# A two-layer decoder on one core: gMLP's v first in each layer, norms by token halves, gates one branch ahead

## What is computed

```python
for l in range(DEPTH):
    h = rmsnorm(x, attn_norm_gain[l])
    q, k, v, pz, gu, gv, g = jnp.split(h @ w_in[l], SPLIT_POINTS, axis=-1)
    gates = jax.nn.sigmoid(g + b_gate[l]).reshape(B, S, N_BRANCHES, D)
    ya = sliding_window_attention(q, k, v, attn_sinks[l], rel_bias) @ w_branch_a[l]
    yb = multiscale_pool(pz, w_pool[l], pool_scale[l]) @ w_branch_b[l]
    yc = chunked_spatial_gating(gu, gv, gmlp_v_gain[l], w_spatial[l], b_spatial[l]) @ w_branch_c[l]
    x = x + (gates[:, :, 0] * ya + gates[:, :, 1] * yb + gates[:, :, 2] * yc) @ w_out[l]
    h2 = rmsnorm(x, ffn_norm_gain[l])
    x = x + peer_ffn(h2, peer_w_query[l], peer_sub_keys1[l], peer_sub_keys2[l], peer_expert_u[l], peer_expert_v[l])
return rmsnorm(x, final_gain)
```

## Time and profile before

| | us |
|---|---|
| median of 3 runs (2059.02 to 2060.73) | 2060.33 |
| the profiled execution's own time | 2059.37 |
| its span | 2057.6 |
| PE busy | 2017.3 |
| DVE busy | 1469.7 |
| ACT busy | 1057.9 |
| POOL busy | 1028.4 |

### The profile page before, as it was taken

The page is one execution under the profiler, slowest core; times in us unless marked ns, Lnnn a source line. Parts: engine busy times, 40 slices in busy tenths (PEclk is TensorE's granted clock), DMA queues, the critical chain, the costliest instruction groups (busy, mean ns, idle before and its releaser), DMA issues.

```text
span 2057.6 us, 41405 instructions
## 1 busy us (share of the span) xinstructions
PE 2017.3 (98%) x13730; PEld 1874.1 (91%) x13730; DVE 1469.7 (71%) x2984; ACT 1057.9 (51%) x1751; POOL 1028.4 (50%) x427
## 2 busy tenths in 40 slices
PE   7999999999999999999989999999999999999997
PEld 6999899999998888889889999999999988888896
DVE  3943169688887888886649341796888778888775
ACT  5644454577774333334365444546777733333343
POOL 5798679877770000004368886797777600000042
PEclk9999999999999999999999999999999999999999
DMA  7455557665667777876454554576565677787763
GB/s 260 135 185 185 173 180 228 223 199 194 196 198 227 242 240 241 242 242 218 162 186 144 187 188 169 187 229 217 195 199 195 195 238 241 241 242 240 233 215 122
DMA packets 164486, 423.36 MB, mean 206 GB/s; under 512 B 18075, under 2 KB 76620, under 8 KB 163868
## 3 DMA queue, kind: packets, MB, share of 16 engines
q1 hardware_dynamic: 163724, 418.24, 63.3%
q10 hardware_dynamic: 288, 2.10, 0.2%
q0 software_dynamic: 368, 1.57, 0.2%
HBM read 388.29 MB, written 33.55 MB: 205 GB/s over the span
## 4 chain that ended last, share of the span: by engine, by line
PE 93%; issue 2%; POOL 2%; ACT 1%; DVE 1%; DMA 0%; DVEq 0%; POOLq 0%; ACTq 0%
PE bank L1112 53%; PE bank L1313 34%; PE bank L1364 3%; POOL halves L463 2%; PE bank L1291 1%; DVE hT L792 0%; PE bank L1274 0%; PE bank L1134 0%; PE bank L1213 0%; ACT area L505 0%; DMA x<-in_x 0%; ACT halves L528 0%; DVE area L785 0%; ACT area L559 0%; PE bank L1223 0%
## 5 line engine op out<-in xcount | busy, mean ns | idle before, releaser
L463 POOL TENSOR_TENSOR halves<-ring,halves 128x1024 fp32r<-128x1024 f32 x412 | 1021.8, 2490 | 992.7 <-DVE coef L1045 617.7
L528 ACT ACTIVATE halves<-ring 128x1024 fp32r<-128x1024 f32 x668 | 705.3, 1057 | 759.5 <-PE bank L1313 408.2
L1112 PE MATMUL bank<-hT,halves 128*128 128x256 f32 x8736 | 1081.5, 283 | 10.2 <-DVE hT L792 9.3
L1112 PEld LDWEIGHTS bank<-hT,halves 128*128 128x128 f32 x8736 | 1063.8, 192 | 16.2 <-DVE hT L792 10.8
L1313 PE MATMUL bank<-halves,coef 128*128 128x512 f32 x3072 | 703.0, 389 | 0.0
L1313 PEld LDWEIGHTS bank<-halves,coef 128*128 128x128 f32 x3072 | 574.4, 188 | 118.6 <-issue 0.5
L1027 DVE TENSOR_TENSOR halves<-ring,halves 128x1024 fp32r<-128x1024 f32 x256 | 315.8, 1234 | 10.4 <-ACT halves L528 10.0
L1039 DVE TENSOR_TENSOR act<-act,area 128x256 f32<-128x256 f32 x256 | 157.5, 615 | 58.8 <-ACT act L641 55.8
L1043 DVE CAST coef<-act 128x256 fp32r<-128x256 f32 x256 | 75.4, 294 | 100.8 <-PE bank L1313 98.0
L690 ACT ACTIVATE onehot<-onehot,weight 128x128 fp32r<-128x128 f32 x256 | 89.1, 395 | 108.2 <-DVE onehot L1010 108.1
L1004 DVE TENSOR_TENSOR onehot<-bank,ids 128x512 fp32r<-128x512 f32 x128 | 88.6, 692 | 48.5 <-PE bank L1364 48.5
(11 more groups left out here) (149 smaller groups left out, 1070.6 us busy)
## 6 DMA issues: line engine op xcount, KB each, us to landing
ring<-in_stream SPq DMA_DIRECT2D x672, 512.0 KB, 3.7
held_blocks<-act SPq DMA_DIRECT2D x220, 128.0 KB, 1.8
act<-held_blocks SPq DMA_DIRECT2D x220, 128.0 KB, 2.9
area<-rel_scratch SPq DMA_DIRECT2D x2, 1024.0 KB, 6.2
x_home<-x ACTq DMA_DIRECT2D x2, 1024.0 KB, 4.2
x<-x_home SPq DMA_DIRECT2D x2, 1024.0 KB, 8.0
rel_scratch<-act POOLq DMA_DIRECT2D x1, 1532.0 KB, 14.7
area<-in_consts SPq DMA_DIRECT2D x2, 576.0 KB, 3.8
```

The lines of the kernel that those rows point to most:

```text
L463: pool.tensor_tensor(halves[:, s, 1, :], ring[:, s, :], halves[:, s, 0, :].bitcast(F32), ALU.subtract)\
L528: a.activation(halves[:, s, 0, :], ring[:, s, :], ACT.Copy).then_inc(hi_done, 1)
L1112: i = pe.matmul(o, stationary[a], moving[b], start=begin and n == 0, stop=end and n == len(TERMS) - 1)
```

## The change

- **Order of a layer.** gv comes first (tiles 2 to 5), by token halves: PE transposes half 0, starts its gv products, transposes half 1. Then k, v, q, the logits, pz, gu, and the four tiles of gate 0 where gv and gu were. After the mixers each gate runs one branch ahead (gate 1, branch 0, gate 2, branch 1, ..., gate 5, branch 4, branch 5); gate 0 has a buffer of its own.
- **Norms by halves.** DVE scales x by 1/rms and by the gain (loaded spread over all partitions, `gain_a`, `gain_f`) into `hn`; PE transposes with the identity (L1274 of the new kernel), ACT and DVE split straight from PSUM. ACT's root, DVE's scaling and PE's transposes alternate between the halves.
- **wo.** Tiles 4 to 7 run for half 0 first, then 4 to 6 for half 1, the transposes of half 0, tile 7 for half 1, five products by the identity, the transposes of half 1.
- **End of PEER.** The last two u tiles stand together, and the last three v tiles are added for half 0 first, then for half 1; the last coefficients have a buffer of their own. x is added and normed by halves here too.
- **Parameters** are no longer tiles of the stream: they are one DMA (`par`), after the bias in layer 0, before the end of the layer in layer 1. POOL makes the four masks after low half 19. The bias table is written from SP's queue, not POOL's; x arrives as two DMAs from two queues.
- **POOL waits** in layer 1 before low halves 3 and 4 until DVE has scaled half 0 and half 1.

The core of the diff:

```diff
-    [("h1T", "V")] * 4 + [("kv", "A")] + [("q", "A")] * 2 + [("vt", "A")] + [("lg0", "V")] * 2 + [("lg1", "V")] * 4
-    + [("pz", "V")] * 2 + [("gv", "A")] * 2 + [("gu", "A")] * 2 + [("pT0", "A")] * 2 + [("pT1", "A")] * 4
+    [("h1T", "V")] * 4 + [("gv", "A")] * 2 + [("kv", "A")] + [("q", "A")] * 2 + [("vt", "A")] + [("lg0", "V")] * 2
+    + [("lg1", "V")] * 4 + [("pz", "V")] * 2 + [("gu", "A")] * 2 + [("gate", "A")] * 2
+    + [("pT0", "A")] * 2 + [("pT1", "A")] * 4 + [("attn", "A")] * 4 + [("gmlp", "V")] * 2 + [("pool", "V")] * 2
...
+                    sp.wait_ge(rel_vector, 1)
+                    sp.dma_start(scratch.rearrange("h (r i) d -> (h r) i d", i=HEADS),
+                                 relv.unsqueeze(1).to_broadcast([P, HEADS, NDIST])).then_inc(rel_written, 16)
...
-                pool.wait_ge(params_ready, l + 1)
+                pool.wait_ge(hi_done, l * HIS + 1)
                 pool.sem_inc(lo_pool, 2)
-                low(2, 2, l)
+                subtract(2)
+                if l > 0:
+                    pool.wait_ge(hn_ready, 8 * l + 2)
                 low(3, 3, l)
-
+                if l > 0:
+                    pool.wait_ge(hn_ready, 8 * l + 4)
+                with pool.Fori(1, 5) as r:
+                    for s in range(RING):
+                        low(r * RING + s, s, l)
+
+                pool.wait_ge(params_loaded, l * 16 + 16)
                 pool.wait_ge(maps_loaded, l * 16 + 16)
                 for g in range(GROUPS):
                     i = pool.tensor_tensor(wsp[:, g, :], par[:, C_WSP + g * P:C_WSP + (g + 1) * P], tril, ALU.mult)
                 i.then_inc(wsp_ready, 1)
-                with pool.Fori(1, T_PV // RING) as r:
+                with pool.Fori(5, T_PV // RING) as r:
...
                 for blk, lg in ((0, lg0), (1, lg1)):
-                    high_up_to(T_GV + 2 * blk)
+                    high_up_to(T_PZ + 2 + 2 * blk)
...
+                def normed(n, t, gain):
+                    rstd(n + t, 2 + t, 4 + t, 1)
+                    for c, cols in enumerate(COLS):
+                        v.scalar_tensor_tensor(hn[:, t, cols], x[:, t, cols], stat[:, 4 + t:5 + t], gain(c),
+                                               ALU.mult, ALU.mult).then_inc(hn_ready, 1)
...
+                for n in range(4):
+                    tile(T_WO + n, 2)
+                    pe.wait_ge(merged_ready, l * 4 + WO_ORDER[n][1] + 1)
                     for t in range(TT):
...
+                        projected(n, t, t == 0)
+                pe.wait_ge(merged_ready, l * 4 + 4)
+                for n in range(4, 8):
+                    tile(T_WO + n, 2)
+                    projected(n, 0, n == 4)
+                for n in range(4, 7):
+                    projected(n, 1, n > 4)
+                transpose_rows("h2T", 4, 0)
+                projected(7, 1, True)
+                for n in range(KEEPERS):
+                    pe.matmul(bank[7][:, 0:S], ident, ids[:, :], start=True, stop=True)
+                transpose_rows("h2T", 4, 1)
...
+                v_half(0, coef[:, 1], 0)
...
+                v_half(1, coef[:, 0], 0)
...
+                v_half(3, coef_last, 0).then_inc(acc_done, 1)
+                v_half(3, coef_last, 1).then_inc(tiles_used, 1)
+                v_half(0, coef[:, 1], 1).then_inc(tiles_used, 1)
+                v_half(1, coef[:, 0], 1).then_inc(tiles_used, 1)
```

More of the change, by code:

```diff
@@ L564, in _ @@
+                a.wait_ge(scal, scaled[0])
+                a.activation(stat[:, 8:10], stat[:, 6:8], ACT.Sqrt, bias=eps, scale=1.0 / (GROUPS * P))\
+                    .then_inc(root_ready, 1)
                 high_up_to(T_V + 3)
@@ L739, in _ @@
                 main(end + 2, 3, NK - 2)
-                main(end + 4, 1, NK - 1, last=True)
-            roots(NSCAL * DEPTH, lambda i: a.wait_ge(x_ready, 4 * DEPTH + (i + 1)))
+                a.wait_ge(tiles_used, l * NT + NT - 3)
+                a.wait_ge(coef_ready, l * NK + NK - 2)
+                gelu(1)
+                a.activation(stat[:, 13:14], one, ACT.Sqrt)
+            for t in range(TT):
+                root(t, lambda c: a.wait_ge(x_ready, 4 * (DEPTH - 1) + 2 * t + c + 1))
         @block.vector
@@ L810, in _ @@
+                lows("h1T", 1)
+                g[0] = first("gv")
+                rstd(3, 8, 10, 2)
+                for t in range(TT):
+                    i = v.tensor_scalar(gv[:, t, :], gv[:, t, :], stat[:, 10 + t:11 + t], None, ALU.mult)
+                i.then_inc(vhat_ready, 1)
+                v.wait_ge(params_loaded, l * 16 + 16)
                 v.wait_ge(bias_loaded, l * 16 + 16)
@@ new lines, in transpose_rows, with rows_ready @@
+                        i.then_inc(groups_done, 1)
+                def rows_ready(name, count):
+                    return l * NGV + taken_before(place(name, count - 1) + 1)[0]
+                if l == 0:
+                    pe.wait_ge(ones_ready, 1)
+                    pe.wait_ge(gain_a_loaded, 16)
+                    for c in range(2):
+                        i = pe.matmul(gain_0[c][:, :], ones, gain_a[0:1, COLS[c]], start=True, stop=True)
+                    i.then_inc(gain_spread, 1)
@@ new lines, in _, with projected @@
+                for kind, n in MIX[1:]:
+                    (gates if kind == "gate" else branch)(n)
+                b = [[group_at(place("wo", 2 * t + hf)) for hf in range(2)] for t in range(TT)]
+                def projected(n, t, opens):
+                    hf, kq = WO_ORDER[n]
+                    w = halves[:, (T_WO + n) % RING].rearrange("p h (k c) -> p h k c", k=2)
+                    for k in range(2):
+                        rows = [merged_h[:, e, 2 * kq + k, t * P:(t + 1) * P] for e in range(2)]
+                        one, i = product(b[t][hf][:, :], rows, (w[:, 0, k], w[:, 1, k]), kq == 0 and k == 0,
+                                         kq == 3 and k == 1)
+                        if opens and k == 0:
+                            one.then_inc(tiles_used, 1)
+                    if kq == 3:
+                        i.then_inc(groups_done, 1)
```

638 lines of the change are left out of this document (365 added, 273 removed).

## The result

| | us |
|---|---|
| before, median of 4 runs (2059.02 to 2060.73) | 2059.82 |
| after, median of 4 runs (2082.45 to 2084.68) | 2084.03 |
| after : before, with its 95% interval | 1.0116 (1.0099 to 1.0134) |
| after, the profiled execution's own time; its span | 2084.68; 2082.9 |

What follows compares the result with a forecast made beforehand. The prediction took PE, busy 98% of the span, as the bound. Its terms, -8.5 - 4.2 + 1.5 + 0 + 19 = +7.8, on the profiled 2059.37 gave 2067, with a range of 2053 to 2076.

Steps and rivals of the forecast that it cites:

- Between the layers: From layer 0's last products through gv, once: norms by halves shorten the stretch, -8.5 (bounds -10 to -6).
- End: After PE's last product, once: adding and norming by halves ends the span 7.3 after it, not 11.5; -4.2.
- Start: Kernel start, once: gv done 1.1 sooner, but later loads delay K and the third Q tile; +1.5 (-2 to +6).
- the rival with 5 more from the SP queue: Layer 0's loads: the SP queue holds K and Q back by 5 more than forecast, 2072; chance 0.1.
- wo to h2T: From wo to Q's products, twice: hidden half 0 norm gains 1.9, earlier need of merged halves costs 1.9; 0 each.
- The rival's mechanism: wo stage: POOL's third query tile starts between half 1's scalings, delaying the second by 2.4; +2 each, 2071; chance 0.08.
- Logits to probabilities: From pz to the transposes of probabilities, twice: PE waits for POOL's late low halves; +9.5 each, +19.
- POOL limits the next tiles anyway: After tile 17's wait: half clock, some 1.4 more per layer, counted only in the upper bound since POOL limits later tiles.
- POOL keeps up: Logits-to-probabilities stage: turns with DVE cost POOL little, only 2.5 lost per layer; -6.2, 2053; chance 0.22.
- late by half: Logits-to-probabilities stage: POOL late by only some 5 to 6 per layer; about 0 in all, 2060; chance 0.2.

Runs made afterwards that it cites:

- Experiment 10: Changed kernel, but DVE waits for all four accumulators before adding the first half of a layer's result: 2093.51, ratio 1.0159.
- experiment 1: Changed kernel with ACT's wait before the sigmoids of gates 3, 4 and 5 moved behind the high halves: 2068.29, ratio 1.0038 to the kernel before.
- experiment 6: Changed kernel with ACT's gate wait moved, plus the third query tile's high half behind half 1's rows on ACT: 2063.58, ratio 1.0016.
- experiment 4: Changed kernel, but ACT makes the high halves of tiles 17 and 18 between the second block's exponentials: 2079.67, ratio 1.0093.
- experiments 7: Changed kernel with ACT's gate wait moved, plus wo's fifth tile done for both halves first: 2068.20, ratio 1.0030.
- 8: Changed kernel with gate wait moved, masks behind tile 23, high halves 17 and 18 between exponentials, later query high half, wo's fifth tile whole: 2051.08, ratio 0.9955.

## Why the prediction was right and wrong

The sign was right. The size was not: 7.8 forecast, 24.2 measured.

1. *Between the layers*, -8.5: **right**, -9.3. gv's end lies 16.3 after the last product (1062.5, the logits less the 18.2 that k, v and q take in both kernels), forecast 17.0. Experiment 10 shows that the halves carry at least 4.7 of it.
2. *End*, -4.2: **right**, 7.3 after the last product as forecast; without halves 11.4.
3. *Start*, +1.5: **right**, +1.8, as far as its scatter allows. PE waits 1.70 and 1.89 for k and the third q tile, forecast 1.5 and 1.2, so the rival with 5 more from the SP queue did not come.
4. *wo to h2T*, 0 each: **mis-sized**, +2.2, and 1.5 to 2.3 at half clock behind it. By itself it is 0 (31.4 against 31.5 in experiment 1). The surplus came in part from the stage ahead, whose late low halves delayed the merged quarter by 0.85; the rest is half clock in layer 0, and in layer 1 the turn that DVE lost to POOL. That the step by itself is 0 was luck: two errors cancelled. The rival's mechanism, the third query tile's low half between half 1's scalings, does occur (a wait of 2.17; 2.4 per layer with the half clock, experiment 6). And each half's transposes, put at 1.87, take 1.03 (8 products by the identity at 231.95).
5. *Logits to probabilities*, +9.5 each: **close**, +8.3. The wait at 17 was 5.6 for 6.0 forecast, and for the forecast reason. What followed was not as forecast: the masks and turns were to cost 3.6 at tile 20, but cost 0.3 and 1.0. In their place stood the half clock, 2.6 and 1.9 for three tiles in the two layers, in whose shadow POOL caught up. (The Trainium skill, TensorE: Matmul & The Clock Gate, Part 1, has the array idle at half rate; the rows agree, at 2.6 and 1.9 where 1.4 was put on it.) "POOL limits the next tiles anyway" held the two for one and the same delay, and that is what the rows show: taking away the masks alone or the wait alone shortened the two stages by 2.0 and 0.9, both together by 11.4.
6. **The step that failed is one that the prediction doesn't have.** Its sum has no term for the gates and branches: it stopped at the mixers and took "each gate runs one branch ahead" for free. A gate ahead has to wait for its sigmoid buffer, since gates 1 to 5 share two; the diff puts that wait in front of the high halves, and ACT serves its queue in order. Three stalls per layer, 10.3 in the stage and 15.7 with what hung on them (some 1.5 of it is the turn that DVE lost in layer 1, which need not hang on them). With that wait moved, the kernel takes 2068.3, where 2067 had been forecast. That close an agreement is luck in part. By the spans of that run step 5 was forecast too high by 2.4 and step 1 by 0.8; against them stand what was forecast too low or not at all, the start by 0.9, the half clock behind wo's transposes by 2.0 and PEER by 1.2.

Of the rivals, "POOL keeps up" and "late by half" fell with step 5. None held a second stage on the same resource; the range was built around one.

What a better version is worth: with the moved wait, masks, two high halves, the query tile, wo's fifth tile and POOL's hold the kernel takes 2048.7, 0.55% less than before (0.41 to 0.69), and keeps what the change gains at its ends.

## What to carry to other kernels

When work is run one step ahead, look for the wait on the buffer that it needs, and for what stands behind that wait on its engine: work that doesn't need the buffer goes first. Cost every stage in which the slower of two coupled producers appears, not only the one where it is last now. And where two losses lie in one chain, removing one of them tells little, since the second stands in its place; try them together before calling either small.

## What was not expected of the hardware

- Short waits cost more than their length, by an amount that differs. After the wait of 5.63 the clock was at its lower level for over 5 us (0.50 in 74.8 to 80), and three tiles lost 2.6; after that of 5.65 in layer 1 they lost 1.9. After the waits of 1.50 in the gates nothing was lost (72 products in 8.90). After 2.51 before wo's fifth tile it was low in layer 0 and full in layer 1 (windows of after, the products right behind that wait; PEclk is the third number from the end):

```profile
220.70:223.00 2.30, 2.30 (x6) 1.84 (x7) 0.00 (x0) 1.52 (x2) 0.41 (x1) 0.51 0.69 224
1250.00:1253.00 3.00, 3.00 (x13) 2.48 (x14) 0.00 (x0) 2.51 (x3) 1.40 (x1) 1.00 0.48 175
```

- DVE's operation with a single SBUF operand (L966, 8 numbers by a constant) waited for a low half (2.33) just as those with two did, while the reciprocals of 8 numbers took 0.20 in every place, beside POOL too (74.37 in experiment 4).
- Two engines that come to the same moment make executions of one kernel differ. Half 0's second scaling and a low half of POOL start within 0.1 of each other in experiments 1, 6 and 7. Where POOL goes first, DVE's two scalings take 3.6 instead of 1.4. The times in experiments 7 and 8 fall into groups 4 to 5 apart; that this turn makes them is likely but not shown, since only one execution of each was profiled.
